# Leaving out the unread products inside the attention loops of a two-block transformer kernel

## The reference

```
att:  8 heads of 64, 256 queries, own and earlier chunks, with a bias     (block 1, layer 0)
mem0: 4 heads of 64, 256 queries against 256 memory keys                  (block 2, layer 0, beside RWKV)
mem1: the same                                                            (block 2, layer 1)
dil:  4 heads, each over three dilation groups, softmax over all three    (block 2, layer 1)

s = q @ k.T (+ bias);  p = exp(s - max);  o = (p / sum(p)) @ v
```

## Time and profile before

| | |
|---|---|
| median of 3 runs | 2271.23 us (2265.87, 2271.23, 2271.84) |
| profiled execution | 2266.92 us, its span 2265.1 us |
| around the span | 1.8 us |
| busy share of PE, DVE, ACT | 96%, 62%, 45% |
| mean granted TensorE clock | 0.983 of full speed (2.4 GHz) |

### The profile page before, as it was taken

How to read it: one execution, slowest core, us unless ns; L and a number is a source line. 1 busy time by engine, 2 the same in 40 slices (tenths; PEclk the granted TensorE clock), 3 DMA queues, 4 the chain that set the end, 5 groups by cost and what they waited for, 6 DMA issues and landing times.

```text
span 2265.1 us, 33265 instructions
## 1 busy us (share of the span) xinstructions
PE 2164.1 (96%) x14214; PEld 1776.8 (78%) x14214; DVE 1406.4 (62%) x1456; ACT 1030.6 (45%) x1155; POOL 74.6 (3%) x138
## 2 busy tenths in 40 slices
PE   6998899999999899999999999989999999999999
PEld 4777777678787777678788897778888888887887
DVE  5767745589775744399756555466556675635664
ACT  4344322367545423277544445335445444535443
POOL 2030000000000000000000000000000000020000
PEclk9999899999999899999999998999999999999999
DMA  9863869999670859999555550006555556433553
GB/s 345 317 201 133 296 243 371 369 337 364 211 260 1 277 187 318 332 340 362 193 191 186 181 176 9 3 6 221 188 187 168 192 177 203 148 92 122 194 186 112
DMA packets 267314, 475.62 MB, mean 210 GB/s; under 512 B 9424, under 2 KB 151824, under 8 KB 262944
## 3 DMA queue, kind: packets, MB, share of 16 engines
q1 hardware_dynamic: 256128, 431.81, 55.2%
q0 software_dynamic: 11040, 41.70, 5.5%
HBM read 471.33 MB, written 2.14 MB: 209 GB/s over the span
## 4 chain that ended last, share of the span: by engine, by line
PE 85%; DVE 7%; ACT 4%; DMA 2%; issue 2%; POOL 0%; ACTq 0%; DVEq 0%; POOLq 0%
PE psum L1069 14%; PE psum L1071 7%; PE psum L1086 3%; PE psum L1088 3%; PE psum L1087 3%; PE psum L1037 3%; PE psum L1039 3%; PE psum L1038 3%; PE psum L1361 3%; PE psum L1406 3%; PE psum L1362 2%; PE psum L1363 2%; PE psum L1518 2%; PE psum L1520 2%; PE psum L1519 2%; DVE w_lo L2798 2%
## 5 line engine op out<-in xcount | busy, mean ns | idle before, releaser
L2798 DVE TENSOR_TENSOR w_lo<-ring,w_hi 128x2048 fp32r<-128x2048 f32 x267 | 609.8, 2289 | 283.2 <-ACT w_hi L2149 277.1
L2149 ACT ACTIVATE w_hi<-ring 128x2048 fp32r<-128x2048 f32 x267 | 510.9, 1915 | 358.5 <-PE psum L1088 119.8
L1069 PE MATMUL psum<-h_both,w_hi 128*128 128x512 f32 x1408 | 499.4, 399 | 1.6 <-DVE h_both L3490 1.3
L1071 PE MATMUL psum<-h_both,w_lo 128*128 128x256 f32 x1408 | 395.1, 281 | 0.0
L1069 PEld LDWEIGHTS psum<-h_both,w_hi 128*128 128x128 f32 x1408 | 264.5, 188 | 68.2 <-issue 1.7
L1071 PEld LDWEIGHTS psum<-h_both,w_lo 128*128 128x128 f32 x1408 | 265.9, 189 | 1.4
L2798 DVE TENSOR_TENSOR w_lo<-pool,w_hi 128x2048 fp32r<-128x2048 f32 x70 | 160.4, 2291 | 112.0 <-ACT w_hi L2149 111.5
L2149 ACT ACTIVATE w_hi<-pool 128x2048 fp32r<-128x2048 f32 x70 | 134.1, 1916 | 168.9 <-DMA pool<-in_exp_w_up 61.6
L2171 ACT ACTIVATE pool<-psum 128x512 f32<-128x512 f32 x88 | 52.6, 598 | 261.1 <-PE psum L1071 261.1
L1037 PE MATMUL psum<-w_hi,h_both 128*128 128x512 f32 (+1 forms) x352 | 141.1, 401 | 6.9 <-DVE h_both L2808 3.2
L1361 PE MATMUL psum<-h_both,w_hi 128*128 128x256 f32 x480 | 139.1, 290 | 0.7 <-DVE w_lo L2798 0.7
(11 more groups left out here) (476 smaller groups left out, 3796.5 us busy)
## 6 DMA issues: line engine op xcount, KB each, us to landing
ring<-in_ffn_pre_w_in SPq DMA_DIRECT2D x44, 1024.0 KB, 5.1
ring<-in_ffn_post_w_in SPq DMA_DIRECT2D x44, 1024.0 KB, 5.1
pool<-in_exp_w_up SPq DMA_DIRECT2D x40, 1024.0 KB, 8.0
ring<-in_exp_w_gate SPq DMA_DIRECT2D x36, 1024.0 KB, 7.7
ring<-in_exp_w_down SPq DMA_DIRECT2D x30, 1024.0 KB, 7.4
ring<-in_ada_w SPq DMA_DIRECT2D x24, 1024.0 KB, 7.0
ring<-in_ffn_pre_w_out SPq DMA_DIRECT2D x22, 1024.0 KB, 5.0
ring<-in_ffn_post_w_out SPq DMA_DIRECT2D x22, 1024.0 KB, 4.9
```

The source lines that it names most:

```text
L1069: pe.matmul(o.rearrange("p (s n) -> p s n", s=2), wh[:, k, fs], h_both[:, :, k, :], start=k == 0, stop=False, skip_group_check=True)
L1071: m = pe.matmul(o[:, 0:T], wl[:, k, fs], h_hi[:, k, :], start=False, stop=k == KD - 1, skip_group_check=True)
L2149: act.activation(w_hi[:, (s["split"] + r) % 3, :], piece(s["pieces"][r]), ACT.Copy)\
L2798: dve.tensor_tensor(w_lo[:, slot, :], piece(s["pieces"][r]), w_hi[:, slot, :].bitcast(F32), ALU.subtract).then_inc(sem("w_lo"), 1)
```

## The change

The two calls of `warm` inside the loop of `attention` on PE are removed. The products outside of the loops stay, and no other engine's program changes.

```
                         if J2 > 1:
                             pe.wait_ge(sem("att_o"), J2 - 1)
-                        if kind in ("mem0", "mem1") or j >= len(jobs):
-                            warm(2 if j == 2 else 1, 6 + j % 2)
                         pe.wait_ge(sem("att_pts"), J2 + 1)
...
                         elif J1 > 1:
                             pe.wait_ge(sem("att_pts"), J1 - 1)
-                        if kind in ("mem0", "mem1"):
-                            warm(3 if j == 1 else 1, 4 + (j - 1) % 2)
                         pe.wait_ge(sem("att_exp"), J1 + 1)
```

## The result

The changed kernel is slower: 2274.76 us median (2267.16 to 2283.93, 8 runs) against 2266.27 us (2264.23 to 2271.84, 8 runs) for the kernel before, ratio 1.0033, 95% interval 1.0018 to 1.0047. The forecast was 2269.3 us, 0.1% less than before, with 6 in 100 for slower by over 0.3%. The base was off too: the first three runs of the kernel before have a median of 2271.23, all eight one of 2266.27. So 2274.76 us lies within the stated range, 2264.0 to 2276.0, by luck: the base was 5 us too high, and the change is +8.5 us where -1.9 was forecast.

The account below looks back on a forecast made before the run. The prediction took PE, busy 96% of the span, as the bound. Terms for att 0, mem1 -2.6, mem0 -0.1 and dil with the tails +0.8 summed to -1.9 us: 2271.2 to 2269.3 us, range 2264.0 to 2276.0.

Parts of the forecast that it names:

- mem1: -2.6 us. The clock is 1.00 throughout.: Loop mem1: leaving out eleven products gains 2.6 us at full clock, bounds 0 and 5.4; dil passes the gain on.
- The rebuilt order of waits: Loop mem1, turn by turn without products: T(0) stays, PV(0) starts at 2012.1, PV(3) at 2018.65 in place of 2021.25.
- The clock falls in mem1 too: +3.5.: Rival for mem1 and dil's start: half speed gives +3.5 in place of -2.6 us, 2275.4 in all; chance 0.20.
- dil's first 3.4 us at half speed cost 1.7: Start of dil, if the clock falls in mem1: only the first 3.4 us run at half speed, costing 1.7 us.
- mem0: -0.1 us.: Loop mem0: line 945 starts 2.7 us earlier, but half speed there gives back all but 0.1; bounds -2.7 and +0.9.
- An execution of the kernel before that kept full clock in mem0 would be 4 to 5 us better there: Remark on mem0 in the kernel before: full clock there would beat the profiled execution by 4 to 5 us.
- mem0's terms: Loop mem0: PV 1.36 us at 1.2 GHz, line 945 2.7 us earlier, lines 945 and 947 costing 2.6 us more.
- att: nothing at the same clock.: Loop att: leaving out two products ahead of PV(6) and PV(7) gains 0, as both waited for ACT's copy.
- At the end of att I find room: End of att: a clock loss is covered, since the next matrix product waits for DVE's splits well after the transposes.
- Tail of dil, +0.8: End of dil: three products at half speed take 1.3 us more, 0.5 covered, so +0.8 us; bounds 0 and +3.
- The clock comes back only in lines 945 and 947: Behind mem0: full clock returns only within the dense stretch of these lines, estimated 5.5 us after its start.
- the third rival: The clock falls in mem1 too and the kernel is slower: +4.2 us with the rest, 2275.4 us; chance 0.20.

Follow-up runs that it names:

- e9_mem0_fit: Changed kernel with nine products back in mem0, three ahead of T(0) and six ahead of PV(0); 2273.98 us, ratio 1.0032 to the kernel before.
- e3_mem1: Kernel before with only mem1's eleven products left out; 2267.63 us, ratio 1.0011.
- e5_dense: Changed kernel with eight unread products added in a row between mem1 and dil; 2274.54 us, ratio 1.0043 to the kernel before.
- e2_mem0: Kernel before with only mem0's eleven products left out; 2266.95 us, ratio 1.0017.
- e1_tails: Kernel before with only the four products in the last two turns of att and dil left out; 2265.79 us, ratio 1.0005.
- e8_att: Kernel before with products added in waits of att, mem0 and dil, and six of mem1's left out; 2264.34 us, ratio 0.9990.
- e4_mem1_first: Kernel before without eight of mem1's eleven products, keeping the three ahead of T(0); 2267.77 us, ratio 1.0007.

## Why the prediction was wrong, point by point

- **"mem1: -2.6 us. The clock is 1.00 throughout."** This step failed. The rebuilt order of waits was right: PV(0) 1.4 us behind T(0), and T(0) to PV(3) in 8.3 us (forecast 7.95, so 2.2 us of the 2.6) in the executions that kept the clock. But the kernel before kept it because of the products. It fell in five of the six profiled executions that left out at least eight of mem1's eleven (kept in e9_mem0_fit's), and in none of the eight that kept more. Where all eleven were out, none stood ahead of dil and the clock fell, T(0) to dil's last PV took 10.5 to 10.7 us more (three profiles). By the medians the place is worth +3.2 us (e3_mem1, ratio not told apart from 1), since not every execution loses the clock there.
- **"The clock falls in mem1 too: +3.5."** The right rival, with too small a price and chance (0.20). Its first part was right (dil's first L +2.5, forecast +1.8 with PV(3) included). "dil's first 3.4 us at half speed cost 1.7" was wrong: dil stays at half speed for 18 us of its 40 and costs 8.2. I had taken a PE that is busy in the profile for one that brings the clock back. e5_dense shows the difference: eight 128x256 products did it within 6.0 us, dil's own turns, with PE busy all of 18.35 us, did not. That the rival's time, 2275.4, is next to the 2274.76 measured is luck: its sum was +4.2 us on a base 5 us too high, where +8.5 was measured.
- **"mem0: -0.1 us."** The base failed: the sum came from the first profile, whose mem0 was the worst of six. From PV(0) to line 1731 the other five take 22.0 to 23.6 us and the four without mem0's products 25.5 to 26.1. So leaving the products out costs 2 to 4 us here, and e2_mem0 alone is +0.17%, the only one of the three places whose interval excludes 1. The text named this ("An execution of the kernel before that kept full clock in mem0 would be 4 to 5 us better there"), then left it out of the sum.
- **mem0's terms, against the first profile.** Line 945 was to start 2.7 us earlier, counted from PV(0), and started 1.0 earlier. A PV at half speed takes 1.90 to 1.97 us without a product ahead of it, and the forecast had 1.36 for the later ones: that row spans the rise of the clock at 1408.6. Lines 945 and 947 then gave back 1.65 us and not 2.6, so that line 1711 starts 0.6 us later. That line 1731 starts 1.0 us earlier all the same comes from the half-speed stretch at 1418.9, which the changed kernel didn't have: as near to -0.1 as this is, it is luck.
- **att: nothing at the same clock.** Right as far as it goes, PV(6) and PV(7) waited for C as before. The clock did fall near the end of att in both profiles of the changed kernel, and the transposes behind it took 1.7 us longer. The room there ("At the end of att I find room") did not hold all of it: from the last PV to the matrix product behind att it is 6.9 and 6.7 us, against 5.8 in all three profiles of the kernel before. e1_tails prices att's and dil's four products together at +0.05%, not told apart from 0. **Tail of dil, +0.8:** 0.8 and 0.6 us in the two profiles of the changed kernel (last PV to the matrix product 5.75 and 5.5 us, against 4.95), 0.0, 0.0 and 0.4 in e1_tails, e5_dense and e9_mem0_fit.
- **The clock comes back only in lines 945 and 947:** right. It came back at 1420.7, 3.5 us behind line 945's start; the forecast had 5.5, of which no row shows the 2.1. The forecast read the stretch from 1418.9 to 1422.3 as line 947's alone, but its first 0.8 us was line 1711's. e3_mem1's profile has the cleaner case: half speed from 1416.7 to 1420.1, with nothing on PE but line 947's transposes, and the clock rose on them. In the changed kernel it rose while PE was in line 945, a product with a constant matrix and no transpose.
- **The page on loops that wait.** The Trainium skill, "TensorE: Matmul & The Clock Gate", in its section on HAM oscillation describes a loop that starts each turn at the low clock, because each turn waits for a DMA for longer than its own matrix products take. I gave the third rival 0.20 because of att's waits. The case here is another one: in mem1 PE waits for ACT, 1.53 us at most, and the clock fell all the same. Nor did it swing from turn to turn: it fell once, for 30.7 us.
- **The clock over the whole kernel.** The 18 runs of the changed kernel have a mean clock of 0.977 where the kernel before has 0.985. By a span of 2270 us that is, as an estimate, some 36 us more at half speed (0.008 x 2 x 2270), each of which can cost up to half of itself: enough for the 8 to 13 us measured and the 2 us gained.

What stays open: which part of a turn counts towards the clock, and why the same loop kept it in one execution and lost it in the next. The experiments vary the number and the place of products and not their form. Which share of executions loses the clock in mem1 isn't measured either: one to three executions of each kernel were profiled.

## What to carry to other kernels

Work whose result nobody reads is to be priced by what it holds up, not by what it takes: here 2.2 us of path against 8 us, in the executions that lose the clock, in a loop that doesn't contain it. Where a loop of short matrix products waits in every turn, try to put such work exactly into the waits and to take it out of the path; here the two kernels that did so came out at 0.9993 and 0.9990, at the edge of what can be told. And one profile is one course of the clock: before a stretch at half speed goes into a base, look at a second profile, or at the mean clock of the runs.

## What the hardware showed that I had not expected

- A stretch at 0.50 can outlast almost full PE: 29.14 us busy of 30.70, in three profiles (the changed kernel's two and e3_mem1's).
- With four unread products in the wait of 1.81 us ahead of PV(0) the clock stayed in att (e8_att, one profile), where in twelve of the thirteen other profiles it had fallen within 3 us of PV(0).
- The clock fell at the end of mem1 behind two waits of 0.79 and 0.78 us (e4_mem1_first). With the same two waits, and 1.53 us ahead of T(0) besides, it stayed in e9_mem0_fit's profile, and so it did behind one of 1.43 us in att, in the first profile. The length of the waits alone doesn't decide.
- The clock rose with nothing but transposes on PE (line 947, at 1420.1 in e3_mem1's profile).
